# Expert 0 of a mixture-of-experts stage: gate for all tokens in rows and then gathered, up and down on one 128-token tile, token scales applied behind the products

## The reference, cut to what matters

```python
x = x + memory_cross_attention(...)            # ends in "o" times w_o
h = rms_norm(x, ffn_norm)                      # x * rsqrt(mean(x^2) + eps) * gain
g_prob = softmax(h @ w_group + b_group)        # 4 groups; top 1
e_logits = h @ w_expert + b_expert             # 16 experts in 4 groups of 4; top 2 within the group
for e in range(16):
    hid = silu(h @ w_gate[e]) * (h @ w_up[e])  # 1024 -> 512
    out += combine[:, e:e+1] * (hid @ w_down[e])   # 512 -> 1024
x = x + out
```

## Time and profile before

| what | value |
|---|---|
| median of 3 runs | 1241.64 us (1238.59 to 1244.49) |
| the profiled execution's own time | 1243.32 us |
| its span, first to last instruction | 1241.5 us |
| busy: PE, PEld | 1203.7 us (97%), 1069.0 us (86%) |
| busy: DVE, ACT, POOL | 900.7, 723.0, 117.9 us |
| read from HBM | 253.15 MB, 205 GB/s over the span |
| start of the o 3 unit's turns; start of the router's logits; start of expert 1's gate | 284.42, 291.13, 335.49 us |

### The profile page before, as it was taken

How to read it: one execution, slowest core, us unless ns; L and a number is a source line. 1 busy time by engine, 2 the same in 40 slices (tenths; PEclk the granted TensorE clock), 3 DMA queues, 4 the chain that set the end, 5 groups by cost and what they waited for, 6 DMA issues and landing times.

```text
span 1241.5 us, 18815 instructions
## 1 busy us (share of the span) xinstructions
PE 1203.7 (97%) x7842; PEld 1069.0 (86%) x7842; DVE 900.7 (73%) x960; ACT 723.0 (58%) x839; POOL 117.9 (9%) x137
## 2 busy tenths in 40 slices
PE   6999999999999999999999899999999999999998
PEld 6978997978888787888877788999999998989897
DVE  5897586557778878888889884758766875755554
ACT  4855224454577677776767454667778744544432
POOL 0100000000000000000000100019732520000000
PEclk8999999999999999999999999989999999999999
DMA  7433234515489888898998156533234446455552
GB/s 269 170 128 144 103 127 144 192 68 212 163 325 369 336 322 340 319 366 313 341 340 335 73 179 239 198 105 103 84 122 162 149 136 220 157 196 201 179 197 102
DMA packets 38179, 255.43 MB, mean 206 GB/s; under 512 B 4192, under 2 KB 6368, under 8 KB 10320
## 3 DMA queue, kind: packets, MB, share of 16 engines
q1 hardware_dynamic: 34800, 247.64, 55.2%
q10 hardware_dynamic: 3296, 6.61, 1.5%
HBM read 253.15 MB, written 1.08 MB: 205 GB/s over the span
## 4 chain that ended last, share of the span: by engine, by line
PE 76%; DVE 11%; ACT 7%; issue 3%; POOL 2%; DMA 1%; DVEq 0%; SPq 0%; ACTq 0%; POOLq 0%
PE bank L447 21%; PE bank L449 21%; PE bank L448 21%; DVE r L1795 4%; ACT r L1226 3%; PE bank L457 2%; PE bank L848 1%; PE bank L612 1%; PE bank L1090 1%; POOL f L2639 1%; PE bank L814 1%; PE bank L672 1%; PE bank L711 1%; DVE r L1804 1%; DMA f<-in_weights 1%
## 5 line engine op out<-in xcount | busy, mean ns | idle before, releaser
L1795 DVE TENSOR_TENSOR r<-f,r 128x2048 fp32r<-128x2048 f32 (+2 forms) x239 | 540.9, 2268 | 176.1 <-ACT r L1226 175.7
L447 PE MATMUL bank<-r,r 128*128 128x256 f32 (+5 forms) x1936 | 644.3, 333 | 12.8 <-DVE r L1795 5.8
L449 PE MATMUL bank<-r,r 128*128 128x256 f32 (+5 forms) x1936 | 633.7, 327 | 0.0
L448 PE MATMUL bank<-r,r 128*128 128x256 f32 (+5 forms) x1936 | 633.3, 327 | 0.0
L1226 ACT ACTIVATE r<-f 128x2048 fp32r<-128x2048 f32 (+3 forms) x240 | 453.3, 1891 | 171.6 <-PE bank L449 146.1
L447 PEld LDWEIGHTS bank<-r,r 128*128 128x128 f32 (+4 forms) x1936 | 359.4, 186 | 57.3 <-issue 18.1
L449 PEld LDWEIGHTS bank<-r,r 128*128 128x128 f32 (+4 forms) x1936 | 359.4, 186 | 34.6
L448 PEld LDWEIGHTS bank<-r,r 128*128 128x128 f32 (+4 forms) x1936 | 359.2, 186 | 34.5 <-issue 1.0
L1804 DVE TENSOR_TENSOR r<-f,r 128x512 fp32r<-128x512 f32 (+3 forms) x70 | 52.8, 764 | 30.5 <-ACT r L1762 11.2
L2639 POOL TENSOR_SCALAR f<-f,f 128x128 f32<-128x128 f32 (+1 forms) x64 | 63.8, 1013 | 44.6 <-DVE f L2425 44.6
L457 PE MATMUL bank<-f,f 128*128 128x128 f32 x224 | 32.1, 303 | 8.4 <-DMA f<-in_cst 6.3
(11 more groups left out here) (325 smaller groups left out, 1075.3 us busy)
## 6 DMA issues: line engine op xcount, KB each, us to landing
f<-in_weights SPq DMA_DIRECT2D x216, 1024.0 KB, 4.9
f<-in_weights SPq DMA_DIRECT2D x12, 896.0 KB, 4.7
f<-in_weights SPq DMA_DIRECT2D x8, 672.0 KB, 4.6
f<-in_weights SPq DMA_DIRECT2D x4, 882.0 KB, 5.4
f<-bias_table ACTq DMA_DIRECT2D x1, 2048.0 KB, 13.0
f<-in_mem ACTq DMA_DIRECT2D x1, 1024.0 KB, 4.7
out<-f ACTq DMA_DIRECT2D x2, 512.0 KB, 2.6
f<-in_moe ACTq DMA_DIRECT2D x1, 647.0 KB, 4.7
```

The lines of the kernel that those rows point to most:

```text
L447: e.matmul(o, lh.r, rh.r, start=start, stop=False)
L448: e.matmul(o, lh.r, rl.r, start=False, stop=False)
L449: return e.matmul(o, ll.r, rh.r, start=False, stop=stop)
L1795: e.tensor_tensor(slot_of(n).r, slot_of(n).f, high_of(n).r.bitcast(F32), ALU.subtract).then_inc(s["w_lo"], 1)
```

## The change

1. X is transposed in the order of quarters 0, 2, 1, 3, between the matmuls of the last o unit, and its transposed form is multiplied by the gain alone. `scale_row`, the diagonals and `scaled` go for this norm. The token scale comes in behind: in the bias addition of the logits (`route_group`) and as `scale=` of the silu of expert 0's gate.
2. Expert 0's gate for all 256 tokens is computed in rows: X stationary, the weights moving, 48 matmuls of 512 columns; the ranks stand between the two token halves of the second unit. ACT applies silu to each half (GR) and splits it, DVE makes the low part, and `gather_gate` gathers expert 0's rows by four matmuls of 512 columns with PA.
3. Expert 0's up and down work on tile 0 like those of experts 1 to 19: `tile_in("up", 0)`, `turn_hidden(0)`, `tile_out(0)`; the down units of expert 0 move behind expert 1's up units. `gather(0)` moves ahead of up. The separate `add_back(2, ...)` and `comb` go.
4. On DVE the XM low part and `tiles` come ahead of `route_experts`; the low part of gate 1 comes behind the norm instead of ahead of it.

```diff
-            add_back(1, [("o", j) for j in range(4)], o_lhs)
-            for a in range(4):
-                turn_added(3, 1, a)
-            scale_row(3)
+            add_back(1, [("o", j) for j in range(4)], o_lhs, 3)
...
+            def gate_rows():
+                bs = [in_bank(("gate", "rows", i), "ev_a", READ_AT["rows", i]) for i in range(2)]
+                def part(kk, i):
+                    t = slice(128 * i, 128 * i + 128)
+                    return mm3(banks[bs[i]][:, :], XH[:, 4 * u + kk, t], XT[:, 4 * u + kk, t], wh[:, kk, :], wl[:, kk, :], u + kk == 0, u + kk == 4)
+                for u in range(2):
...
+                    if u == 0:
+                        for kk in range(4):
                             logits(kk)
+                            for i in range(2):
+                                m = part(kk, i)
+                    else:
+                        for i in range(2):
+                            for kk in range(4):
+                                m = part(kk, i)
+                            if i == 0:
+                                full["rows"] = done(m)
+                                ranks()
...
+            def gather_gate():
+                b = take("gg")
+                for i in range(2):
+                    e.wait_ge(s["gr"], i + 1)
+                    for src in (GRH, GR):
+                        m = e.matmul(banks[b][:, :], PA.r[:, i, 0:128], src.r[:, i, :], start=i == 0 and src is GRH, stop=i == 1 and src is GR)
...
-            dense_in("gate", "ev_a", READ_AT["silu", 0])
...
-            dense_in("up", "ev_d", READ_AT["hid", 0])
+            gate_rows()
             e.wait_ge(s["xn_l"], 1)
             e.wait_ge(s["pa"], 1)
+            gather(0)
+            rotation[1] += 2
+            tile_in("up", 0, "ev_d", READ_AT["hid", 0])
+            gather_gate()
             e.wait_ge(s["cmb"], 1)
-            gather(0)
-            add_back(2, [("down", 0), ("down", 1)], dense_lhs)
+            turn_tile(0)
...
 # ScalarE
-            for a in range(4):
-                e.wait_ge(s["x_add"], added(1, a))
-                square(3, X, a)
-            turn_high(3)
+            high_and_square(3, 3, 1)
             e.dma_start(FB, fng).then_inc(s["l_f"], 16)
+            ahead(("gate", 0))
             e.wait_ge(s["pe_done"], full["rl"])
             e.activation(LGT[0:20, :], banks[bank_at["rl"]][0:20, 0:256], ACT.Copy).then_inc(s["r_lg"], 1)
-            ahead(("gate", 0))
...
+                read_out(("rows", i), e.activation(GR.f[:, i, :], banks[bank_at["gate", "rows", i]][:, :], ACT.Silu, scale=rows[3][i][5]))
+                e.activation(GRH.r[:, i, :], GR.f[:, i, :], ACT.Copy).then_inc(s["gr_h"], 1)
...
 # VectorE
-            add_and_turn(1, ("o", 3), 3)
+            add_and_take(1, ("o", 3), 3)
...
-                e.tensor_tensor(LG, banks[bank_at["rt"]][:, 0:40].rearrange("p (i n) -> p i n", i=2),
-                                S("br").unsqueeze(1).to_broadcast([128, 2, 20]), ALU.add).then_inc(s["r_bi"], 1)
+                for i in range(2):
+                    m = e.scalar_tensor_tensor(out=LG[:, i, :], in0=banks[bank_at["rt"]][:, 20 * i:20 * i + 20], scalar=rows[3][i][5], in1=S("br"),
+                                               op0=ALU.mult, op1=ALU.add)
```

More of the change, by code:

```diff
@@ L25 @@
 TILES = 5
-OUT2 = 3 + TILES
+OUT2 = 2 + TILES
 EXPERTS = 4 * TILES
@@ L42, in unit_plan @@
         add(t, range(2 if t in ("hf", "hq", "hi", "hg", "cc", "cx", "cb") else 4))
-    for t in ("gate", "up", "down"):
-        add(t, range(2))
-    for e in range(1, EXPERTS + 1):
+    for e in range(EXPERTS + 1):
         if e < EXPERTS:
@@ L284, in build @@
         LGT = room(256)
-        HGD = room(1024).rearrange("p (c t) -> p c t", c=4)
-        HH, HI = (room2(1024).re("p (c t) -> p c t", c=4) for _ in range(2))
+        GR, GRH = (room2(1024).re("p (i f) -> p i f", i=2) for _ in range(2))
         HG, HD = ([room(512) for _ in range(2)] for _ in range(2))
@@ L794, in dense_in, with ranks @@
                 let_go()
+            def ranks():
+                b = take("rk")
+                e.wait_ge(s["oh"], 1)
+                e.wait_ge(s["l_g"], 16)
+                ohs = [oh[:, i, :] for i in range(2)]
+                e.matmul(banks[b][:, 0:4], tri, ohs[0], start=True, stop=True)
+                e.matmul(banks[b][:, 4:8], C("ones"), ohs[0], start=True, stop=False)
+                e.matmul(banks[b][:, 4:8], tri, ohs[1], start=False, stop=True)
+                e.matmul(banks[b][:, 8:12], C("ones"), ohs[0], start=True, stop=False)
+                full["rk"] = done(e.matmul(banks[b][:, 8:12], C("ones"), ohs[1], start=False, stop=True))
+                freed[b] = ("pa", 1)
+            def gather_gate():
[4 more added lines that the diff above has]
+                        m = e.matmul(banks[b][:, :], PA.r[:, i, 0:128], src.r[:, i, :], start=i == 0 and src is GRH, stop=i == 1 and src is GR)
+                full["gg"] = done(m)
+                freed[b] = ("ev_a", READ_AT["silu", 0])
             def tile_in(name, x_, evac, release):
@@ L1465, in _ @@
             gathered(0)
-            ahead(("down", 0))
-            ahead(("down", 1))
+            e.wait_ge(s["sv_d"], 4)
+            e.activation(s1[:, 3, :], s1[:, 3, :], ACT.Exp).then_inc(s["sv_a"], 1)
+            for i in range(2):
+                if i == 0:
+                    e.wait_ge(s["pe_done"], full["rows"])
+                else:
+                    wait_unit(("gate", 1))
+                e.wait_ge(s["n_rs"], SCALES[3] + i + 1)
+                read_out(("rows", i), e.activation(GR.f[:, i, :], banks[bank_at["gate", "rows", i]][:, :], ACT.Silu, scale=rows[3][i][5]))
+                e.wait_ge(s["ev_a"], READ_AT["rows", i])
+                e.activation(GRH.r[:, i, :], GR.f[:, i, :], ACT.Copy).then_inc(s["gr_h"], 1)
+            ahead(("up", 1))
+            e.wait_ge(s["pe_done"], full["gg"])
+            read_out(("silu", 0), e.activation(HG[0], banks[bank_at["gg"]][:, :], ACT.Copy))
             for x_ in range(1, EXPERTS):
@@ L2245, in _ @@
             route_group()
-            ahead(("gate", 1))
-            route_experts()
             e.wait_ge(s["xn_h"], 1)
@@ L2579, in scales @@
             def scales(r):
-                order = ORDER if r in (2, 5) else range(4)
+                order = ORDER if r in (2, 3, 5) else range(4)
                 for i in range(2):
```

163 lines of the change are left out of this document (57 added, 106 removed).

## The result

| what | before | after |
|---|---|---|
| median, runs on one chip | 1242.6 us (6 runs, 1238.59 to 1245.41) | 1227.63 us (6 runs, 1223.38 to 1230.11) |
| ratio, 95% interval | 1 | 0.9875 [0.9856, 0.9893] |
| the profiled execution's own time | 1243.32 us | 1228.05 us |
| its span, mean granted clock | 1241.5 us, 0.990 | 1226.2 us, 0.992 |

A forecast was written before the change was run, and what follows sets the result against it. PE, busy for 97% of the span, was taken as the bound. The terms -3.2 - 1.7 + 0.2 - 5.8 - 5.6 + 1.4 + 1.2 gave -13.5 us, a median of about 1228, with an 8-in-10 range of 1224 to 1233.5.

The forecast's parts named there:

- The way into the router: Last o product to first logits: half the transposes move into the last o unit, 3.5 us for 6.7, -3.2 us.
- Low clock: Clock of 0.50 from 292.0 to 295.4, behind the old 2.41 us gap, taken as gone: -1.7 us, bounds -1.7 and 0.
- Gate, up, down: Expert 0's matmuls at 0.231 us per 512 columns: gate +0.2, up -5.8, down -5.6 us.
- Added work: New on PE: `gather_gate` 0.9 us, expert 0's `turn_hidden` 0.44, a little at their edges: +1.4 us.
- Waits: PE waiting at ranks 0.2, gather 1.0, `gather_gate` 0.5, less 0.20 and 0.30 that go: +1.2 us, bounds 0 and +5.
- VectorE's walk: DVE's steps from the norm's low parts (291.3) through the one-hot groups (299.3) to PA (304.2).
- The routing chain: Rival: late up 0 weights delay the logits' copy, ranks and PA; gain only 6 to 8 us, 1234 to 1236; chance 0.17.
- the bad end of what the rival named: Routing chain, four weight units landing together at 299.7: 5.7 us lost, perhaps 1.7 of clock too.
- The low clock staying: Rival: low clock at the same place or behind new waits; gain 11.8, 1229.9; 0.3 within the forecast's share.
- The stock of weights: Rival: experts lived on six stored units worth 18.7 us; kernel 5 us slower, 1247; chance 0.02.

The follow-up runs named there:

- e4: Changed kernel plus two VectorE additions (some 2.4 us) between XM's low part and `tiles()`; 1232.32 us, 0.9927 of before.
- e2: Changed kernel with the old norm (transposes behind the last o unit, scale matmuls, scaling on DVE); 1229.65 us, 0.9897 of before.
- e3: Changed kernel in which PE waits for all of the norm's low parts ahead of the first logits; 1230.56 us, 0.9911 of before.
- e7: Kernel before the change with four slots for weights throughout; 1277.23 us, 1.0279 of before.

## Why the prediction was right, point by point

1. *The way into the router, -3.2.* From the stage's first point to the first logits it was 9.45 us before and is 6.42 after: -3.0. The logits start at 289.28, or 288.1 without the 1.18 us that the trace is late ahead of the stage; predicted 287.9.
2. *Low clock, -1.7.* Right: 1.00 from 288 to 336. It held by a margin that I had not priced. The longest wait left is 0.47 us, and e4 shows that one of 2.72 us brings 3.2 us of low clock.
3. *Gate, up, down: +0.2, -5.8, -5.6.* The price of 0.231 us for 512 columns moved held: up takes 5.65 us, and expert 0's down ends at 333.43 (332.2 without the shift, near 333 as predicted). The Trainium skill's 131 ns (TensorE: Matmul & The Clock Gate, Back-to-back issue gap) would have made the saving 5 us smaller; the trace does not bear it out.
4. *Added work, +1.4.* The four matmuls of `gather_gate` are 0.92, as said (1.16 with their wait, which belongs to the next point); `turn_hidden(0)` took 0.36 and not 0.44.
5. *Waits, +1.2.* This was the term that was mis-sized. It had 0.2 at the ranks, 1.0 at the gather and 0.5 at `gather_gate`, less 0.20 and 0.30 that went. Measured 0, 0.47 and 0.24 less the same, so +0.2 (+0.4 if the gather's is taken from start to start, 0.65). VectorE's walk was exact up to PA: last low parts done at 292.7, or 291.5 shifted (predicted 291.3), groups at 299.4 (299.3), PA at 304.1 (304.2). The step that failed is PE's own arrival: without the shift it reached the ranks at 299.66 and not 299.1, and would have reached the gather at 303.5 and not 303.1 to 303.3. The first logits were 0.2 late, and from there to the ranks it took 11.56 us, where the walk had 11.2: small edges between matmuls of different widths that it left out. Being late cost nothing there, since PE would have waited. At `gather_gate` GR's second low part was done at 313.95 and not 314.5.

Behind these, 1.3 us in experts 2 to 19 had no term at all. Sum: -13.5 predicted, -14.3 in the stage and -15.3 in the profiled execution. The median fits to 0.4 us, but partly by luck: the six runs spread over 6.7 us, in step with their mean clocks (1223.4 and 1223.5 at 0.995 and 0.996, 1229.7 and 1230.1 at 0.988). Over all eleven runs of the changed kernel the median is 1226.8.

*The rivals.* The routing chain: up 0's high part started at 293.11, the first of the four units queued; had it been the last, the loss would by e4 have been nearer to the bad end of what the rival named, since low clock came on top there. The low clock staying: not in this stage. The stock of weights: SP waits for PE as before. Its waits after, 420 to 680 us, against the earlier trace rows:

```profile
SPq L2689 <- PE bank L446: 224.8, 80, 12.0
```

## What to carry to other kernels

When an expensive dense step is replaced by a shorter one, walk the other engine's chain to the next point where they meet; the gain lasts only until that chain binds, and here it already bound by half a microsecond. A wait of PE has two prices, itself and the clock behind it, and the second can be the larger. Compare small variants side by side on one chip, and by the length of the stretch that was edited: measured apart, the version with fillers was 3.8 us under the changed kernel; side by side it was 1.8 above it, which five runs of each do not tell from no difference.

## What the runs showed of the hardware

- **The low clock is partly chance.** With norm 3's gap (before, e2, e3, e7) and with e4's wait at the gather, 2.4 to 3.3 us idle, it followed in 5 of 5 traces, and in the stage it never came in the 9 traces without such an idle time or with it filled. But at norm 4, where the idle time is 2.7 us, the clock fell in it or just behind it in 6 of the 11 traces that leave it unfilled (0 of 3 filled), and at the 1.5 us near 187 in 7 of 13. Each such place costs 1.5 to 3.4 us, which is the spread of the runs.
- **It also follows small matmuls without idle time.** It fell in all 14 traces at a run of 64 float32 matmuls of 64x15, between 2.4 us ahead of the run's end and 0.7 us behind it, with no idle time of PE over 0.1 us in the 19 us ahead of the fall. In the trace after, windows around them (800.37 to 804.95, PE busy throughout):

```profile
800.00:803.00 3.00, 3.00 (x52) 2.86 (x50) 0.00 (x0) 1.88 (x2) 0.00 (x0) 1.00 0.46 131
803.00:806.00 3.00, 3.00 (x25) 2.96 (x26) 0.85 (x3) 0.00 (x0) 0.00 (x0) 0.50 0.53 224
```

  The Trainium skill (TensorE: Matmul & The Clock Gate, Part 1) ties the two levels to how busy the array has been. The filled gaps agree with it; a busy share of 3.00 in 3.00 ahead of a fall does not follow from it by the profile's measure of busy.
- **A slot of weights is held longer than its parts.** 13.4 us per cycle of four against 11.7 of landing, splits and use. Six slots cover the rest; five were not tried.
